# Gathering the chosen expert rows of 64 of 288 tokens in a one-core decoder layer

## The reference

```python
s1 = einsum('thd,hkd->thk', q[..., :half], keys[:, 0])     # 8 heads, 128 keys
s2 = einsum('thd,hkd->thk', q[..., half:], keys[:, 1])
v1, i1 = top_k(s1, 16); v2, i2 = top_k(s2, 16)
cand = (v1[..., :, None] + v2[..., None, :]).reshape(T, 8, 256)
vs, ic = top_k(cand, 16)
idx = e1 * 128 + e2                    # 16 of 16384 experts for each head and token
g = softmax(vs)
act = gelu(einsum('thkd,td->thk', U[idx], c)) * g
out = einsum('thk,thkd->td', act, V[idx])
```

## Time and profile before

| | |
|---|---|
| Time, median of 3 runs | 3019.31 us (3018.59 to 3023.04) |
| Span of the profiled execution | 3016.9 us |
| PE busy, span share | 2834.0 us, 94% |
| DVE busy | 1717.4 us, 57% |
| ACT busy | 1213.0 us, 40% |
| POOL busy | 2.5 us |
| DMA | 389.29 MB, mean 129 GB/s |

### The profile page before, as it was taken

How to read it: one execution, slowest core, us unless ns; L and a number is a source line. 1 busy time by engine, 2 the same in 40 slices (tenths; PEclk the granted TensorE clock), 3 DMA queues, 4 the chain that set the end, 5 groups by cost and what they waited for, 6 DMA issues and landing times.

```text
span 3016.9 us, 53624 instructions
## 1 busy us (share of the span) xinstructions
PE 2834.0 (94%) x19564; PEld 2661.5 (88%) x19564; DVE 1717.4 (57%) x3311; ACT 1213.0 (40%) x2023; POOL 2.5 (0%) x18
## 2 busy tenths in 40 slices
PE   8999946899899998799999999999999999999997
PEld 6677734669799997699999999999999999999887
DVE  2289895566658887933333333335555555555466
ACT  1200002213344446944444444444444444444443
POOL 0000000000000000000000000000000000000000
PEclk9799977779899999999999999999999999999999
DMA  6124412226543331033333333344445544444543
GB/s 163 56 91 132 139 56 86 87 84 182 157 133 125 125 129 66 0 125 127 137 125 126 136 127 125 132 151 166 166 167 167 164 155 162 162 166 166 171 112 115
DMA packets 218075, 389.29 MB, mean 129 GB/s; under 512 B 21348, under 2 KB 167396, under 8 KB 200676
## 3 DMA queue, kind: packets, MB, share of 16 engines
q1 hardware_dynamic: 218020, 388.56, 39.0%
HBM read 374.04 MB, written 14.49 MB: 129 GB/s over the span
## 4 chain that ended last, share of the span: by engine, by line
PE 78%; DVE 14%; issue 4%; ACT 2%; DVEq 1%; DMA 0%; ACTq 0%
PE ps L389 11%; PE ps L390 11%; PE ps L391 11%; PE ps L1182 9%; PE ps L1185 9%; PE ps L1181 9%; PE ps L1113 7%; PE ps L261 3%; PE ps L812 1%; PE ps L1723 1%; DVE work L544 1%; DVE work L547 1%; DVE work L539 1%; DVE work L540 1%; DVE work L541 1%
## 5 line engine op out<-in xcount | busy, mean ns | idle before, releaser
L389 PE MATMUL ps<-ffn_h,part_h 128*128 128x288 f32 x2176 | 685.8, 315 | 14.8 <-issue 10.3
L390 PE MATMUL ps<-ffn_l,part_h 128*128 128x288 f32 x2176 | 642.3, 295 | 0.0
L391 PE MATMUL ps<-ffn_h,part_l 128*128 128x288 f32 x2176 | 639.1, 294 | 0.0
L1181 PE MATMUL ps<-act_h,v_high 128*128 128x288 f32 x2048 | 551.8, 295 | 6.1 <-DVE act_l L1418 3.6
L1182 PE MATMUL ps<-act_l,v_high 128*128 128x288 f32 x2048 | 552.2, 295 | 0.0
L1421 DVE TENSOR_TENSOR v_low<-ring,v_high 128x1024 fp32r<-128x1024 f32 x256 | 313.8, 1226 | 372.1 <-ACT v_high L1292 372.1
L1214 ACT CAST part_h<-ps 128x512 fp32r<-128x512 f32 x512 | 299.7, 586 | 466.1 <-PE ps L1113 465.4
L445 DVE TENSOR_TENSOR part_l<-ps,part_h 128x512 fp32r<-128x512 f32 x368 | 254.0, 691 | 404.9 <-ACT part_h L1214 402.4
L389 PEld LDWEIGHTS ps<-ffn_h,part_h 128*128 128x128 f32 x2176 | 409.8, 188 | 18.0 <-issue 16.2
L390 PEld LDWEIGHTS ps<-ffn_l,part_h 128*128 128x128 f32 x2176 | 412.0, 189 | 0.0
L391 PEld LDWEIGHTS ps<-ffn_h,part_l 128*128 128x128 f32 x2176 | 409.7, 188 | 0.0
(11 more groups left out here) (339 smaller groups left out, 3212.2 us busy)
## 6 DMA issues: line engine op xcount, KB each, us to landing
ring<-in_peer_u SPq DMA_DIRECT2D x128, 1024.0 KB, 5.3
ring<-in_peer_v SPq DMA_DIRECT2D x128, 1024.0 KB, 5.6
ring<-in_w_in SPq DMA_DIRECT2D x20, 2048.0 KB, 8.0
ring<-in_w_out SPq DMA_DIRECT2D x16, 1024.0 KB, 5.9
ring<-in_w_ple_gate SPq DMA_DIRECT2D x16, 1024.0 KB, 5.9
out<-work SPq DMA_DIRECT2D x37, 256.0 KB, 3.2
work<-in_state_mlstm_C SPq DMA_DIRECT2D x32, 256.0 KB, 4.9
ring<-in_peer_w_q SPq DMA_DIRECT2D x8, 1024.0 KB, 5.7
```

Source lines behind the costliest of these rows:

```text
L389: pe.matmul(bank, w_h, rhs_h, start=start, stop=False)
L390: pe.matmul(bank, w_h, rhs_l, start=False, stop=False)
L391: return pe.matmul(bank, w_l, rhs_h, start=False, stop=stop)
L1181: pe.matmul(ps[c][:, 0:T], w_h, a_h, start=st_, stop=False)
```

## The change

`PACKS = 2`, `N = T - 64 = 224`. The last 64 tokens leave the dense work. The dense parts (all Ua, Ub and V matmuls, the gelus, gates, casts and subtractions of activations, and the spread, now 14 rounds) work on 224 columns. The table streams, transposes and splits of the tables stay as they are. The three token blocks of the top-k become `PTOK` = (224..287), (0..127), (128..223).

For the 64 tokens GpSimd issues 8 + 8 small block copies that lay indices and gates out as 64 columns of 128 numbers (a column holds four of a token's 32-number groups for 32 tokens), 6 copies that repeat the 64 tokens' activations on all partition groups (`cnat`), and 64 + 64 indirect transfers of 128 rows of 8 KB (1 MB) from U and V into two slots `got`. The activations of those tokens are turned to token order on PE in four groups (`cnat_done`) and copied by ACT before the exp. On DVE a multiply-and-sum of two halves of 1024 stands for each gathered U column among the subtractions of Ub, in the 64 tiles after the first; and a multiply-and-add of two halves for each gathered V column among those of V. PE sums over the partition groups with `pick` at the end, and DVE adds these sums. Some semaphores are merged under new names, since their number is limited.

```diff
+PACKS = 2
+N = T - 32 * PACKS
+PTOK = [(N, 32 * PACKS), (0, 128), (128, N - 128)]
+GATHERS = 32 * PACKS
+DOT_PAIRS = GATHERS // 2
...
-                m = three(pe, ps[4 + s][:, 0:T], q, k, rhs_h[:, k, :], rhs_l[:, k, :], (q, j) == (0, 0), (q, j) == (3, 3))
+                n = N if name in ("Ua", "Ub") else T
+                m = three(pe, ps[4 + s][:, 0:n], q, k, rhs_h[:, k, 0:n], rhs_l[:, k, 0:n], (q, j) == (0, 0), (q, j) == (3, 3))
...
                     o.do(v.tensor_tensor(part_l[:, q, :], src, part_h[:, q, :].bitcast(F32), ALU.subtract),
                          sem("low_done"))
+                    if dots is not None and isinstance(i, int) and q % 2 == 0 and 0 < 2 * i + c <= 2 * DOT_PAIRS:
+                        dots(2 * i + c - 1, q // 2)
...
+        def pool_rows(pool):
+            pool.wait_ge(sem("irow_ready"), 1)
+            for i in range(PACKS):
+                for g in range(4):
+                    pool.dma_start(gidx[32 * g:32 * g + 32, 32 * i:32 * i + 32],
+                                   irow_u[32 * i:32 * i + 32, 32 * g:32 * g + 32]).then_inc(sem("sel_in"), 16)
+            pool.wait_ge(sem("sel_in"), 16 * 4 * PACKS)
+            def fetch(table, n):
+                pool.indirect_dma_start(got[n % 2], None, ins[table][0],
+                                        bass.IndirectOffsetOnAxis(ap=gidx[:, n:n + 1], axis=0)).then_inc(
+                    sem(f"row_in{n % 2}"), 16)
+            fetch("peer_u", 0)
+            fetch("peer_u", 1)
+            pool.wait_ge(sem("tok3_ready"), 1)
+            for i in range(PACKS):
+                for g in range(4):
+                    pool.dma_start(ggate[32 * g:32 * g + 32, 32 * i:32 * i + 32],
+                                   tok3[32 * i:32 * i + 32, 0, 2, 32 * g:32 * g + 32]).then_inc(sem("sel_in"), 16)
+            pool.wait_ge(sem("cnat_copied"), 4 * PACKS)
...
+            for n in range(2, GATHERS):
+                pool.wait_ge(sem("dot_done"), 2 * (n - 1))
+                fetch("peer_u", n)
+            for n in range(GATHERS):
+                if n < 2:
+                    pool.wait_ge(sem("dot_done"), 2 * (GATHERS - 1 + n))
+                else:
+                    pool.wait_ge(sem("row_added"), 2 * (n - 1))
+                fetch("peer_v", n)
...
+            for b in range(4):
+                if b >= 2:
+                    pe.wait_ge(sem("cnat_copied"), PACKS * (b - 1))
+                for j in range(4):
+                    k = 4 * b + j
+                    to = ps[6 + b % 2][0:32 * PACKS, j * P:(j + 1) * P]
+                    pe.matmul(to, ffn_h[:, k, N:T].bitcast(F32), ident[:], start=True, stop=False)
+                    m = pe.matmul(to, ffn_l[:, k, N:T].bitcast(F32), ident[:], start=False, stop=True)
+                m.then_inc(sem("cnat_done"), 1)
...
-                            pe.matmul(ps[c][:, 0:T], w_h, a_h, start=st_, stop=False)
-                            pe.matmul(ps[c][:, 0:T], w_h, a_l, start=False, stop=False)
+                            pe.matmul(ps[c][:, 0:N], w_h, a_h, start=st_, stop=False)
+                            pe.matmul(ps[c][:, 0:N], w_h, a_l, start=False, stop=False)
...
+            pe.wait_ge(sem("row_added"), 2 * GATHERS)
+            for c in range(8):
+                for b in range(2):
+                    for i in range(PACKS):
+                        at = N + 32 * (PACKS * b + i)
+                        m = pe.matmul(ps[c][:, at:at + 32], cnat[i][:, (8 * b + c) * P:(8 * b + c + 1) * P], pick,
+                                      start=True, stop=True)
+                m.then_inc(sem("picked"), 1)
...
+            for b in range(4):
+                act.wait_ge(sem("cnat_done"), b + 1)
+                for i in range(PACKS):
+                    own = slice(32 * i, 32 * i + 32)
+                    o.do(act.copy(cnat[i][own, 512 * b:512 * b + 512], ps[6 + b % 2][own, 0:512]), sem("cnat_copied"))
...
             v.wait_ge(sem("ex3_copied"), 3)
+            v.wait_ge(sem("sel_in"), 16 * 8 * PACKS)
...
+            def dot(n, half):
+                if half == 0:
+                    v.wait_ge(sem(f"row_in{n % 2}"), 16 * (n // 2 + 1))
+                else:
+                    v.wait_ge(sem("dot_done"), 2 * n + 1)
+                cs = slice(1024 * half, 1024 * half + 1024)
+                d = gdot[:, n:n + 1]
+                o.do(v.tensor_tensor_reduce(got[n % 2][:, cs], got[n % 2][:, cs], cnat[n // 32][:, cs], 1.0,
+                                            d if half else 0.0, ALU.mult, ALU.add, d), sem("dot_done"))
+            low_parts(v, o, "Ub", lambda q: ps[q][:, 0:512], gate, {"tile_freed": 2}, dots=dot)
+            v.wait_ge(sem("gdot_gelu"), 1)
+            o.do(v.tensor_tensor(gdot, gdot, ggate, ALU.mult))
+            o.do(v.memset(wk(P * N, 1, PACKS * D)[:, 0, :], 0.0))
...
+            def add_row(i, half, k, part):
+                if part == 0:
+                    v.wait_ge(sem(f"row_in{k}"), i * 16 + (16 * (GATHERS // 2) + 16 * (16 * half + 1)))
...
+                o.do(v.scalar_tensor_tensor(a, got[k][:, cs], gdot[:, ds(i * 2 + (32 * half + k), 1)], a, ALU.mult, ALU.add),
+                     sem("row_added"))
...
                         o.do(v.tensor_tensor(vl[:, s % 2, :], natural[s // 2][:, 1024 * (s % 2):1024 * (s % 2) + 1024],
                                              vh[:, s % 2, :].bitcast(F32), ALU.subtract), sem("vl_done"))
+                        if s % 2 == 0:
+                            add_row(i, half, k, s // 2)
...
+            for c in range(8):
+                for b in range(2):
+                    h = hT[:, 8 * b + c, N:T]
+                    o.do(v.tensor_tensor(h, h, ps[c][:, N + 32 * PACKS * b:N + 32 * PACKS * (b + 1)], ALU.add),
+                         sem("pv_added"))
```

More of the change, by code:

```diff
@@ L434, in high_parts, with low_parts @@
             o.open = {}
-        def low_parts(v, o, name, bank, evac, per, only_first=False, ahead=False):
+        def low_parts(v, o, name, bank, evac, per, only_first=False, ahead=False, dots=None):
             base, _ = TRIPLE[name]
@@ L446, in quarter @@
                          sem("low_done"))
+                    if dots is not None and isinstance(i, int) and q % 2 == 0 and 0 < 2 * i + c <= 2 * DOT_PAIRS:
+                        dots(2 * i + c - 1, q // 2)
             if only_first:
                 quarter(0, 0, 0, 0 if base == 0 else 9)
+                return
+            if dots is not None:
+                quarter(0, 0, 0, 9)
+                for i in range(DOT_PAIRS):
+                    quarter(i, 1, 1, 9)
+                    evac(i, 0, 0)
+                    quarter(i, 2, 0, 9)
+                    evac(i, 1, 1)
+                n = TRIPLE[name][1]
+                with v.Fori(DOT_PAIRS, n // 2 - 1) as i:
+                    o.loop(i, {"low_done": 8, **per})
+                    quarter(i, 1, 1, 9)
+                    evac(i, 0, 0)
+                    quarter(i, 2, 0, 9)
+                    evac(i, 1, 1)
+                    o.leave(n // 2 - 1 - DOT_PAIRS)
+                e = n // 2 - 1
+                quarter(e, 1, 1, 9)
+                evac(e, 0, 0)
+                evac(e, 1, 1)
+                o.open = {}
                 return
@@ L1033, in build @@
         gsum = wk(17152, 2, PH)
-        dense = wk(0, P, T)
+        irow = wk(17168, 1, P)[:, 0, :]
+        irow_u = work[:, 17296:17424].bitcast(U32)
+        dense = wk(0, P, N)
+        cnat = [wk(P * N + 2048 * i, 1, D)[:, 0, :] for i in range(PACKS)]
+        got = [wk(P * N + 2048 * (PACKS + i), 1, D)[:, 0, :] for i in range(2)]
+        gidx = ex3[:, 0, N:T].bitcast(U32)
+        ggate, gdot = ex3[:, 1, N:T], ex3[:, 2, N:T]
+        pick = rs[:, 0:32]
         ohA = [ring[:, 1, 512 * s:512 * s + 512].rearrange("p (a b) -> p a b", b=P) for s in range(4)]
@@ L1361, in dve_peer @@
                     beside(2)
+                if i == 0:
+                    o.settle()
+                    o.do(v.scalar_tensor_tensor(irow[0:n], tok3[0:n, 0, 0, :], float(PK), tok3[0:n, 0, 1, :], ALU.mult, ALU.add))
+                    beside(1)
+                    o.settle()
+                    o.do(v.tensor_copy(irow_u[0:n], irow[0:n]), sem("irow_ready"))
             beside(4 * UA)
-            for i, (t0, n) in enumerate(TOK):
+            for i, (t0, n) in enumerate(PTOK):
                 g = tok3[0:n, i, 2, :].rearrange(hr, r=TK)
@@ new lines, in dve_peer @@
+            low_parts(v, o, "Ub", lambda q: ps[q][:, 0:512], gate, {"tile_freed": 2}, dots=dot)
+            v.wait_ge(sem("gdot_gelu"), 1)
+            o.do(v.tensor_tensor(gdot, gdot, ggate, ALU.mult))
+            o.do(v.memset(wk(P * N, 1, PACKS * D)[:, 0, :], 0.0))
+            o.do(v.tensor_reduce(pick, ident[:].rearrange("p (s t) -> p t s", t=32), AX.X, ALU.add))
+            o.settle()
+            def add_row(i, half, k, part):
+                if part == 0:
+                    v.wait_ge(sem(f"row_in{k}"), i * 16 + (16 * (GATHERS // 2) + 16 * (16 * half + 1)))
```

(17 more changed lines are left out.)

131 lines of the change are left out of this document (71 added, 60 removed).

## The result

The changed kernel takes 2858.74 us (median of 4 runs, 2854.24 to 2866.90) beside 3021.02 us before: ratio 0.947, 95% interval 0.945 to 0.948. The forecast was 2940 us, faster; the time lies 81 us under it, within the range. The profiled execution has a span of 2856.2 us against 3016.9, 160.7 us less, where the prediction's sum had 79.

What follows compares the result with a forecast made beforehand. The prediction took PE's matmul stream to bound about 1860 us (Ub, V, Ua). Its terms summed to -79 us from 3016.9, 2938, and with the median 2.4 above the span 2940 us; range 2800 to 3120, the forecast's own 2850 to 3005.

Steps and rivals of the forecast that it cites:

- The step of a narrow matmul: On PE, a 224-column matmul was to take 0.111 us, bounds 0.103 and 0.132, in place of 0.132.
- Ub's term: In Ub, 92 tiles at 7.12 us in place of 8.13 were to save 93 us, bounds -128 and 0.
- The dots: DVE's multiply-and-sums of 1024 in Ub, two in each of 64 tiles, were to take 1.28 us each.
- The gathers in Ub: Gathers for the Ub tiles were to land within the 9.4 us available and cost nothing.
- Ua: Stage Ua was to take 269 us in place of 297: -28 us, bounds -37 and 0.
- Softmax and turn: Between Ua and the spread, ACT's cnat copies and POOL's gate copies were to add 13 us, bounds 8 and 22.
- Ub to V: DVE's small gelu product, memset and sum ahead of the first act_l were to add 5 us, bounds 2 and 6.
- end of V: At V's end, 64 pick records and 16 adds of 64 columns were to add 8 us.
- V: Stage V was to go from 3.18 to 3.34 us a key tile: +40 us, bounds -82 and +212.
- hold 5.84 + L 7.5 = 13.3: Cycle of a natural slot in V: 5.84 us from landing to release plus 7.5 us load, 13.3 us per four key tiles.
- the transfers hardly meet: Rival for V: loads take L = 5.6 us, V changes by -82 us for +40, 2818 us in all; chance 0.17.

Runs made afterwards that it cites:

- narrow192: Changed kernel with all expert work of the last 96 tokens left out and dense work on 192 columns; 2733.82 us, one run.
- no_v_gathers: Changed kernel without the 64 gathers of peer_v; the adds stay and add whatever the buffer holds; 2800.78 us.
- half_loads: Changed kernel with each 1 MB load into a natural slot in V split into two of 512 KB, each waiting only for its own key tile's v_low; 2779.89 us.
- best_pick: Changed kernel with halved loads in V, ACT's exponentials ahead of its cnat copies, and DVE's memset and pick sum moved earlier; 2769.81 us.
- pick_wide: Changed kernel with each of the 64 pick records streaming 128 columns of rs in place of 32; 2852.99 us, one run.
- adds_last: Changed kernel with each gathered row's add moved in DVE's queue from behind a slot's first v_low to behind its second; 2814.38 us.
- tiny_adds: Changed kernel with the gathered rows' adds working on 16 columns of 1024, gathers and waits kept; 2814.88 us.

## Why the prediction was right in direction and 81 us too high

*The step of a narrow matmul*: right. 0.111 was taken from the transposes and the 1-column rows, 0.112 is measured, and narrow192 shows that it doesn't get shorter with fewer columns. Ub's term came out exact. The dots take 1.21 and 1.28 us for 1.28, and DVE is at 70% there for "near 80%". The Trainium skill (TensorE: Matmul & The Clock Gate, LDWEIGHTS) gives 107 ns for the load of 128 columns. The trace nearly agrees: its shortest steps are 111 to 112 ns.

*The gathers in Ub*: hidden, as said. They land in 7.7 us where 9.4 were to be had. The Trainium skill (DMA: Bandwidth & Descriptors, Measured) has 6.15 us for a plain 1 MB transfer from GpSimd, of which it says that the time to make the descriptors isn't counted. The gather of the same size takes 1.5 us more here, a median from its issue on and beside SP's loads.

*Ua*: -20 for -28. DVE is 89% busy in it (241.79 of 271 us), PE 95%. That the top-k paces it a little more than I allowed is my reading; no run tried it alone.

*Softmax and turn, Ub to V, end of V*: +10, +3 and +10 for +13, +5 and +8. The memset is 3.47 us and not 4.3. At the end the picks took 10.44 us and not 7, because of the clock.

*V*: the step that failed is the size of the cycle, "hold 5.84 + L 7.5 = 13.3", and with it V's sign: it got 45 us shorter, not 40 longer. The mechanism was right: the slot's cycle is what PE waits for, and each run that took something from a link of it made V shorter, close to the sum's own number where the loads are regular (no_v_gathers) and to PE's pace where slots were loaded and freed by halves (half_loads). Both sizes were high. L is 6.6 us in the median, not 7.5: I had added two thirds of the 2.9 us by which the longest landing of the trace exceeds the usual one, but the gathers add only 1.0 (5.6 to 6.6). The hold is 5.5 us, not 5.84. Part of that is how I added: recorded lengths end to end, with 0.3 for handovers on top, while in the chain above DVE's next instruction starts 1.20 us after the add began (2117.38 to 2118.58), before the end of its recorded 1.28; the `v_low` ahead of it (1.23) and the `act_l` behind it (0.38) overlap their followers by 0.08 to 0.09 too. With the measured values the prediction's own formula gives 12.1 us a cycle, and 64 x 12.1 = 774 us for 776 measured. The error is 1.2 us in 13.3, times 64 cycles: 77 of the 85 us. The remaining 8 are the yardstick: "3.18 us a key tile" before is 821.2/256 = 3.21 when the whole stage is taken.

This is what made the forecast fragile: PE's 10.8 us lie close under the cycle, so that each 0.1 us in either link is worth 6 us of the kernel. The rival "the transfers hardly meet" had L = 5.6 and 2818 us, near what was seen without the gathers or with the add out of the hold (2801 and 2814), not with both in place. The measured landing, 6.6, lies halfway between the rival's and the forecast's, and the measured time is nearer to the rival's (41 us) than to the forecast's (81 us).

What is left of the way to the 2752 us of the dense work alone: best_pick has V at PE's pace. Its median is 17 us more, its profiled execution 19: 9 at the end of V (the picks), 5 in a later start of V (of which the one-hots, which begin at 1157.43 and not at 1153.56, have 4), 3 in the tail, where the mean granted clock is 0.89 for 0.93, and 2 in V.

## What to carry to other kernels

When one engine's work shrinks, sum the cycle of each buffer under it (landing, every instruction up to the release, the queue in between, the next load) and compare that with the engine's new pace; here a full PE became one with gaps all through V, and the cure was neither fewer bytes nor less DVE work but loads and releases at half the grain. Where the two are close, don't put medians into the sum: take the landing's spread too, since the longer of the two counts each time. And before narrowing a matmul, look for its price in rows with little to stream: going from 224 to 192 columns bought nothing in the products here, so more could be gained in them only by fewer matmuls or a cheaper weight load, which wasn't tried. And a gain in one short stretch can be taken back in the next by the granted clock, as in pick_wide: count it over the whole kernel.

## What the runs showed of the hardware

- fp32r products with 128 weight columns start 0.111 us apart at 192 columns, 0.112 at 224, 0.119 at 256 and 0.132 at 288, all at a granted clock of 1.00.
- The granted clock fell from 1.00 to 0.50 in a run of 32-column matmuls that kept PE 100% busy, and did not fall when the same 64 records streamed 128 columns: 10.44 against 7.31 us. The narrow records made their own stretch slower, but hardly the kernel: with the wide ones the clock fell in the tail instead, which took 2.9 us more.
- POOL's issue of an indirect gather of 128 rows takes 0.94 us in Ub and, in most of V, 1.98 us. The landings go with it, 7.7 and 9.5 us. With the adds moved it is 0.94 us in V too, with a landing of 7.6:

```profile
L1129 POOL DMA_INDIRECT work<-in_peer_v,ex x64: 935/1976/1992, 1698.7 to 2655.4; - x64
```

```profile
L1129 POOL DMA_INDIRECT work<-in_peer_v,ex x64: 932/935/1110, 1700.9 to 2616.7; - x64
```

  The first row is the changed kernel's, the second that of adds_last (min, median and max in ns). The shrunk adds have 1.97 us, and half_loads, with whole adds in their old place, has 0.94. So neither the add's length nor its place decides. What does is whether DVE's `v_low` is running when the issue starts. POOL's and DVE's timelines, first of the changed kernel, then of half_loads:

```profile
2107.20 1.98 POOL L1129 DMA_INDIRECT work<-in_peer_v,ex  x1 [10.05 <-DVE work L1553]
2107.14 1.22 DVE L1564 TENSOR_TENSOR v_low<-ring,v_high 128x1024 fp32r<-128x1024 f32 x1
```

```profile
2113.04 0.94 POOL L1130 DMA_INDIRECT work<-in_peer_v,ex  x1 [9.78 <-DVE work L1553]
2113.42 1.23 DVE L1564 TENSOR_TENSOR v_low<-ring,v_high 128x1024 fp32r<-128x1024 f32 x1 [0.34 <-ACT v_high L1395]
```

  An issue that starts at least 0.03 us after a `v_low` did and before its end lasts until 0.80 to 0.83 us after that end. It was so in 60 of 62 issues in V of the changed kernel, 45 of tiny_adds, 9 of half_loads and none of adds_last; the other 134 of these 248 take 0.93 to 1.11 us. The gathers had time enough in either case.
- 291 GB/s were moved beside a full PE, with DVE at 79% and ACT at 50%, in V with halved loads (2310 to 2540 us of half_loads), and 296 GB/s in Ub (1300 to 1690 us of the changed kernel, DVE at 74%), both at a DMA share of 0.85.
